# x normed ahead of everything, memory rows transposed beside the first output projection

## What is computed

```python
def rmsnorm(x, gain):
    y = x * rsqrt(mean(x * x, axis=-1, keepdims=True) + EPS) * gain

# block 1: gated recurrence heads (a) and forgetting attention heads (b)
h = rmsnorm(x, norm1_gain)
proj = h @ w_in                      # 2048 -> q_a, f_a, i_a, g_a, q_b, k_b, v_b, f_b
x = x + concat([o_a, o_b]) @ w_out   # "out"
h = rmsnorm(x, norm2_gain)
x = x + conv_ffn(h, ...)             # ffn0, down0, ffn1, down1
...
# block 2, both layers: 4-head cross attention into 256 fixed memory rows
mk, mv = split(mem @ w_mem_kv[layer], 2)
```

## Time and profile before

| | |
|---|---|
| median of 3 runs | 2035.94 us (2035.9 to 2038.04) |
| profiled execution | 2034.77 us |
| its span in the trace | 2033.1 us |
| TensorE busy | 2002.6 us |
| VectorE busy | 1239.8 us |
| ScalarE busy | 866.2 us |

### The profile page before, as it was taken

How to read it: one execution, slowest core, us unless ns; L and a number is a source line. 1 busy time by engine, 2 the same in 40 slices (tenths; PEclk the granted TensorE clock), 3 DMA queues, 4 the chain that set the end, 5 groups by cost and what they waited for, 6 DMA issues and landing times.

```text
span 2033.1 us, 24675 instructions
## 1 busy us (share of the span) xinstructions
PE 2002.6 (99%) x10731; PEld 1716.6 (84%) x10731; DVE 1239.8 (61%) x1113; ACT 866.2 (43%) x806; POOL 21.7 (1%) x62
## 2 busy tenths in 40 slices
PE   7999999999999999999999999999999999999998
PEld 6888987888888888888888888888878888888886
DVE  6665556655666664456666545657865864566665
ACT  5444344444544443344444435343344433344542
POOL 2000000000000000000000000000000000000000
PEclk9999999999999999999999999999999999999999
DMA  9755455475665655556555666746485656554552
GB/s 343 231 166 186 126 168 162 146 268 186 196 198 175 207 175 195 190 191 203 181 192 187 249 216 198 230 152 186 151 331 186 217 186 190 185 158 147 193 199 88
DMA packets 295288, 393.22 MB, mean 193 GB/s; under 512 B 6446, under 2 KB 225387, under 8 KB 293515
## 3 DMA queue, kind: packets, MB, share of 16 engines
q1 hardware_dynamic: 292320, 365.19, 55.4%
q0 software_dynamic: 2400, 26.28, 3.3%
q10 hardware_dynamic: 459, 0.16, 0.0%
HBM read 383.22 MB, written 8.39 MB: 193 GB/s over the span
## 4 chain that ended last, share of the span: by engine, by line
PE 93%; DVE 3%; ACT 1%; issue 1%; DMA 1%; SPq 0%; DVEq 0%; ACTq 0%
PE G L383 37%; PE G L387 18%; PE G L428 11%; PE G L430 11%; PE G L429 11%; PE SB L684 1%; DVE hl_ring L353 1%; ACT hl_ring L350 1%; DMA xt<-in_x 1%; PE OB L705 1%; DVE ytmp L634 0%; PE G L448 0%; PE G L450 0%; PE G L449 0%; DVE ringscr L1650 0%
## 5 line engine op out<-in xcount | busy, mean ns | idle before, releaser
L353 DVE TENSOR_TENSOR hl_ring<-raw,hl_ring 128x2048 fp32r<-128x2048 f32 (+1 forms) x348 | 783.9, 2256 | 521.0 <-ACT hl_ring L350 520.6
L350 ACT ACTIVATE hl_ring<-raw 128x2048 fp32r<-128x2048 f32 (+1 forms) x348 | 655.1, 1886 | 587.8 <-PE G L430 309.0
L383 PE MATMUL G<-ahl,hl_ring 128*128 128x512 f32 x2112 | 665.2, 396 | 0.0
L387 PEld LDWEIGHTS G<-ahl,hl_ring 128*128 128x128 f32 x2112 | 396.7, 188 | 93.7
L387 PE MATMUL G<-ahl,hl_ring 128*128 128x256 f32 x2112 | 415.1, 278 | 0.0
L383 PE MATMUL G<-ops,hl_ring 128*128 128x512 f32 x1216 | 384.3, 397 | 1.4 <-DVE hl_ring L353 1.4
L383 PEld LDWEIGHTS G<-ahl,hl_ring 128*128 128x128 f32 x2112 | 322.0, 189 | 0.8 <-issue 0.5
L387 PEld LDWEIGHTS G<-ops,hl_ring 128*128 128x128 f32 x1216 | 228.4, 188 | 53.9
L387 PE MATMUL G<-ops,hl_ring 128*128 128x256 f32 x1216 | 239.1, 278 | 0.0
L383 PEld LDWEIGHTS G<-ops,hl_ring 128*128 128x128 f32 x1216 | 185.6, 189 | 1.9 <-DVE hl_ring L353 1.6
L428 PE MATMUL G<-hl_ring,hhl 128*128 128x512 f32 x352 | 136.9, 389 | 0.0
(11 more groups left out here) (335 smaller groups left out, 1735.8 us busy)
## 6 DMA issues: line engine op xcount, KB each, us to landing
raw<-in_w_in SPq DMA_DIRECT2D x120, 1024.0 KB, 5.4
raw<-in_w_out SPq DMA_DIRECT2D x48, 1024.0 KB, 5.1
raw<-in_w_ffn_gate SPq DMA_DIRECT2D x44, 1024.0 KB, 5.1
raw<-in_w_ffn_up SPq DMA_DIRECT2D x44, 1024.0 KB, 5.1
raw<-in_w_ffn_down SPq DMA_DIRECT2D x40, 1024.0 KB, 5.1
raw<-in_w_kv_shared SPq DMA_DIRECT2D x24, 1024.0 KB, 5.2
raw<-in_w_mem_kv SPq DMA_DIRECT2D x16, 1024.0 KB, 5.2
ahl<-memop_scratch POOLq DMA_DIRECT2D x2, 4096.0 KB, 13.9
```

The costliest lines, as they stand in the source:

```text
L350: eng.activation(hi[:, s, 0:size], raw[:, r, 0:size], ACT.Copy).then_inc(hi_ready, 1)
L353: eng.tensor_tensor(lo[:, s, 0:size], raw[:, r, 0:size], hi[:, s, 0:size].bitcast(F32), ALU.subtract).then_inc(lo_ready, 1)
L383: eng.matmul(G[:, 2 * pair + b, :], hi[:, s, w], p.rhs(k), start=first and q == 0, stop=False)
L387: last = eng.matmul(G[:, 2 * pair + b, 0:TOK], lo[:, s, w], p.rhs(k)[:, 0, :], start=False, stop=final and q == len(ks) - 1)
```

## The change

x is loaded first, in three pieces with a semaphore each, and normed at once: ScalarE takes the squares and a square root in place of logarithm and exponential, VectorE scales the first half and the third quarter, ScalarE the last. The gain of the first norm alone is loaded by ScalarE's queue and transposed ahead; the other vectors come on GpSimd's queue and are transposed after the second tile of `in_f`. The first tile of the kernel is one of `in_f`; groups 4 to 7 of x are turned inside it, through a `hook` before every other step. Memory is loaded into `normx` once the forgetting attention has ended, transposed after the third and fourth tile of `out`, and `mem_k0` runs between `out` and `mem_v0`. The turned memory needs no way back for `mem_v0`.

```diff
-        add("mem_k0", 2, std(A["w_mem_kv"][0], 0), mem_ops)
         add("in_f", 4, std(A["w_in"], HG), act_ops)
...
         add("out", 4, full_source(A["w_out"], 0, (2, 3, 0, 1)), mixed, form="F", tpc=4, mats=turned_mats)
+        add("mem_k0", 2, std(A["w_mem_kv"][0], 0), mem_ops)
...
+            sp.dma_start(xt[:, 0, :], A["x"][0:P, :]).then_inc(x_loaded[0], 16)
+            for i in range(2):
+                w = slice(i * 1024, (i + 1) * 1024)
+                sp.dma_start(xt[:, 1, w], A["x"][P:2 * P, w]).then_inc(x_loaded[1 + i], 16)
+            for p in order:
                 sp_phase(sp, p.name)
...
+            pool.wait_ge(s_o, HH)
+            for t in range(TT):
+                pool.dma_start(normx[:, t, :], A["mem"][t * P:(t + 1) * P, :]).then_inc(mem_loaded, 16)
             pool.wait_ge(mem_lo, 8)
-            pool.wait_ge(tile_used, 2)
             pool.dma_start(memop, memhl[:, :, :, :].rearrange("p k h t -> p (k h t)")).then_inc(mem_saved, 16)
             phase_over(pool, "mem_k0")
             store(0, 0)
             pool.wait_ge(mem_saved, 16)
-            pool.wait_ge(r_lo, 4)
-            bring_back(memhl)
+            pool.wait_ge(stored, 16)
...
+            pe.wait_ge(x_scaled, 2)
+            pe_turn(pe, 0, 0)
...
+            def first_tile(k):
+                if k and k % 2 == 0:
+                    pe_turn_group(pe, 0, 3 + k // 2)
+                if k % 2 == 0:
+                    pe.wait_ge(t_lo, k // 2 + 1)
+
+            def beside_f(m):
+                if m == 0:
+                    pe_turn_group(pe, 0, 7)
+                if m == 1:
+                    pe.wait_ge(consts, 1)
+                    pe.wait_ge(vec_loaded, 10 * 16)
+                    for v, n in enumerate((124, 105, 88)):
+                        last = pe.transpose(XP[0][:, v * P:v * P + n], vrows[0:n, v, :], ident[0:n, 0:n])
+                    last.then_inc(vec_t, 1)
...
+            def beside_out(m):
+                if m not in (2, 3):
+                    return
+                if m == 2:
+                    pe.wait_ge(s_tmp, HH)
+                    pe.wait_ge(mem_loaded, 32)
+                for g in range(4 * (m - 2), 4 * (m - 2) + 4):
+                    if g >= 4:
+                        pe.wait_ge(mem_lo, g - 3)
...
+            act.wait_ge(x_loaded[0], 16)
+            act.activation(normx[:, 0, :], xt[:, 0, :], ACT.Square, accum_out=ssum[:, 0:1]).then_inc(x_square, 1)
+            act.wait_ge(x_square, 1)
+            act.activation(nrs[:, 0, 0:1], ssum[:, 0:1], ACT.Sqrt, scale=1.0 / D, bias=epsr[:, 0:1]).then_inc(x_root, 1)
...
             split(act, True, 0)
+            act.wait_ge(gain_ready, 1)
+            act_turn(act, 0, 0)
+            act_turn(act, 0, 4)
             split(act, True, 1)
...
             split(dve, False, 0)
...
+            dve.wait_ge(gain_ready, 1)
+            dve_turn(dve, 0, 0)
+            dve_turn(dve, 0, 4)
             split(dve, False, 1)
```

More of the change, by code:

```diff
@@ L379, in alternate @@
             for g in range(0, len(order), 2):
+                if hook is not None:
+                    hook(g // 2)
                 for (b, ks, width, col, first, final), q in order[g:g + 2]:
@@ L413, in pe_phase @@
                     if p.form == "A":
-                        last = alternate(eng, p, pair, s, c, t)
+                        last = alternate(eng, p, pair, s, c, t, hook if m == 0 else None)
                     for b, ks, width, col, first, final in p.mats(c, t) if p.form != "A" else ():
@@ L582, in dve_scale, with pe_turn_group @@
                 ins.then_inc(t_xn, 1)
+        def pe_turn_group(eng, u, g):
+            if u == 0 and g == 4:
+                eng.wait_ge(x_rest, 1)
+            if u and g == 0:
+                eng.wait_ge(t_xn, 2 * u)
+            if g >= 4:
+                eng.wait_ge(t_y if u == 3 else t_lo, g - 3 if u == 3 else 8 * u + g - 3)
+            for k in range(2):
+                for t in range(TT):
+                    kk = 2 * g + k
+                    last = eng.transpose(XP[g % 4][:, k * 256 + t * P:k * 256 + (t + 1) * P],
+                                         normx[:, t, kk * P:(kk + 1) * P], ident[:, :])
+            last.then_inc(t_t, 1)
         def pe_turn(eng, u, first):
             for g in range(first, first + 4):
[L587 to L596, removed]
+                pe_turn_group(eng, u, g)
         def act_turn(eng, u, first):
@@ L933, in _ @@
         def _(pe):
[L934 to L951, removed]
+            pe.wait_ge(ident_ready, 1)
+            pe.wait_ge(gain_loaded, 16)
+            pe.transpose(G[:, 3, 0:16], vrows[0:16, 0, :], ident[0:16, 0:16]).then_inc(gain_t, 1)
+            pe.wait_ge(x_scaled, 2)
+            pe_turn(pe, 0, 0)
             def turns(u):
@@ L962, in normed @@
                 return (((t_lo, 8 * u + 4),), ((t_lo, 8 * u + 8),))
-            pe_phase(pe, "mem_k0", between=turns(0))
-            pe_phase(pe, "in_f", halves=normed(0))
+            def first_tile(k):
[12 more added lines that the diff above has]
+                    last.then_inc(vec_t, 1)
+            pe_phase(pe, "in_f", between=beside_f, halves=((), ((t_lo, 8),)), hook=first_tile)
             pe_phase(pe, "in_q")
@@ L1121, in turns, with beside_f @@
                 return beside
[L1123 to L1132, removed]
+            def beside_f(m):
+                if m == 3:
+                    act.wait_ge(lb_chain, 3)
+                    act.activation(lbt[:, 2:4, :], lbt[:, 0:2, :], ACT.Exp).then_inc(lb_exp, 1)
+                    act.wait_ge(fw_loaded, 16)
+                    act.wait_ge(fw_zero, 2)
+                    for j in range(6):
+                        ins = act.activation(fwhi[:, :, j * HH:(j + 1) * HH], fwraw[:, :, :], ACT.Copy)
+                    ins.then_inc(fw_hi, 1)
+            cut_phase(act, True, "in_f", no_evict, between=beside_f)
             def beside_q(m):
@@ L1228, in _, with beside_out @@
                 act.activation(ah[:, 2 * b:2 * b + 2, :], ablk[:, 2 * b:2 * b + 2, :], ACT.Copy).then_inc(r_hi, 1)
-            cut_phase(act, True, "out", squares_evict(act, "out"))
+            def beside_out(m):
+                if m in (2, 3):
+                    for g in range(4 * (m - 2), 4 * (m - 2) + 4):
+                        act.wait_ge(in_t, g + 1)
+                        if g == 0:
+                            act.wait_ge(r_lo, 4)
+                        act.activation(memh[:, 2 * g:2 * g + 2, :], blocks(XP[g % 4]), ACT.Copy).then_inc(mem_hi, 1)
+            cut_phase(act, True, "out", squares_evict(act, "out"), between=beside_out)
             act_rstd(act, 1)
+            cut_phase(act, True, "mem_k0", no_evict)
             cut_phase(act, True, "mem_v0", full_evict(act, "mem_v0", mem_values), between=turns(1))
@@ L1560, in _, with beside_out @@
             lower(3)
-            cut_phase(dve, False, "out", residual_evict(dve, "out"))
+            def beside_out(m):
+                if m in (2, 3):
+                    for g in range(4 * (m - 2), 4 * (m - 2) + 4):
+                        dve.wait_ge(mem_hi, g + 1)
+                        dve.tensor_tensor(meml[:, 2 * g:2 * g + 2, :], blocks(XP[g % 4]),
+                                          memh[:, 2 * g:2 * g + 2, :].bitcast(F32), ALU.subtract).then_inc(mem_lo, 1)
+            cut_phase(dve, False, "out", residual_evict(dve, "out"), between=beside_out)
             dve_scale(dve, 1)
+            cut_phase(dve, False, "mem_k0", kv_evict("mem_k0"))
             cut_phase(dve, False, "mem_v0", no_evict, between=turns(1))
```

180 lines of the change are left out of this document (93 added, 87 removed).

## The result

The changed kernel takes 2045.51 us (median of 5 runs, 2041.92 to 2045.8), the kernel before 2035.94; the ratio is 1.004, 95% interval 1.0029 to 1.005. It is slower, by 9.6 us where 6.6 were forecast, and 0.2 us above the upper end of the range. Seven later runs of the unedited kernel had a median of 2043.0, 6.3 above the kernel before in the same session; the middle of all twelve is 2043.7. So the five recorded runs lie in the upper part of the changed kernel's spread. The profiled execution took 2045.51 with a span of 2043.8, 10.7 more than before.

A forecast was written before the change was run, and what follows sets the result against it. TensorE was taken as the bound. Second tile done at 39.2, plus 22.3, 3.5 and 0.4 owed, less 11.1 for two `in_f` tiles, gives 54.3; less 47.7 is +6.6 us, so 2042.5, range 2039.2 to 2045.3 (+3.3 to +9.4).

The forecast's parts named there:

- the clock's own end: Upper end for the second tile's clock loss: 1.6 us, where 0.8 was taken between 0 and 1.6.
- The landing and the first matmul: At the start, x and the first weight tile land, are normed, cut and turned; first matmul at 18.8, against 18.04.
- the lag: Delay from data moved to usable, 1.6 us on the old first weight tile, assumed again for x and that tile.
- The first tile: First `in_f` tile with 16 transposes of x: 7.3 us, plus 1.6 for half clock, ending at 27.7.
- The wait behind the first tile: TensorE idles 5.1 us before the second `in_f` tile, whose cut stands behind all eight turned groups.
- the three steps named: After the first tile, in sequence: ScalarE's copy of the last group 0.9, ScalarE's second cut 1.9, VectorE's 2.3 us.
- The second tile: Second `in_f` tile: starts at 32.8, 5.57 us plus 0.8 of clock, done at 39.2.
- The owed work: Still due after the second tile: four `mem_k0` tiles 22.3, 32 memory transposes 3.5, vectors' transposes 0.4 us.
- after 1400 the same 16.8 us: Sign expected in the changed profile: TensorE idle after 1400 us stays at 16.8 us.
- Rival 2: Clock kept and loads early at the start, x and tile without lag: +2.6 us, 2038.5; chance 0.14.
- Rival 3: Turning hidden, second cut over by about 25, second tile done at 30.7: -1.9 us, 2034.0; chance 0.04.
- Rival 4: Weights late in `out` under the memory load and write: +12 us, 2048; chance 0.04.

The follow-up runs named there:

- after_hold_out0: Changed kernel with 22 identity transposes in TensorE's wait before the kernel's second output projection ("the projection"): 2042.28 us, ratio 1.0025.
- hold_second: Changed kernel with 40 identity transposes behind the first tile's last turned group, filling TensorE's wait for the second tile: 2041.58 us, ratio 1.0024.
- after_all_hold: Changed kernel with 60 and 28 identity transposes around x's first transposes, 40 before the second tile, 22 before the second output projection: 2038.92 us, ratio 1.0011.
- before_hold_out0: Kernel before the change with 22 identity transposes in TensorE's wait before the kernel's second output projection: 2035.33 us, ratio 0.9995.
- cut2_between: Changed kernel with ScalarE's and VectorE's second weight cut moved between the fourth and fifth turned group of x: 2038.61 us, ratio 1.0013.
- cut2_paced: As cut2_between, and the second tile waits for turned groups one by one instead of all eight at once: 2037.34 us, ratio 1.0002.
- paced_warm: cut2_paced with identity transposes in three waits: 60 before x's first transposes, 28 behind them, 22 before the second output projection: 2033.46 us, ratio 0.9984.
- before_all_hold: Kernel before the change with 14 and 26 identity transposes around the vectors' transposes and 22 before the second output projection: 2036.98 us, ratio 1.0.

## Why the prediction was right, and where a size was off

**The verdict and its cause.** Right in the direction and in the mechanism; the recorded median lies 0.2 us above the range. The change is slower because TensorE, the bound, starts its second tile late and has 3.5 us of transposes more to pay; both are shown by edits that undo or double them. The range itself was loose: its upper end, +9.4, has no row behind it, as the clock's own end gives 6.6 + 0.8 = 7.4.

**The landing and the first matmul**: forecast 18.8, measured 17.96. x came earlier than the lag allowed for: ScalarE's first square starts at 5.91, not 7.2, and the first weight tile is taken at 12.79, not 13.7. The new load moved 221 GB/s until 6 us and 329 until 9, where the old one, with eight small pieces in front, moved 195 and 299; whether the pieces are the reason was not tested. By its own rows, the prediction's 5.6 and 7.2 for the first half should also have been 5.4 and 7.0. The estimate that the prediction took from the Trainium skill ("DMA: Bandwidth & Descriptors") had the tile at 11.6, so the trace lies between the two. Its 2 us stand there, in the section on the anatomy of a DMA, for loads on GpSimd's path, and this load is on SP's queue.

**The first tile**: 7.3 us of work and 1.6 of clock were forecast, 10.1 measured (17.96 to 28.1), so 2.8 of clock. The old first tile as a row for the clock was mis-sized, since how long the half rate lasts is not the same from start to start: in after_hold_out0 the same tile took 9.2, and in hold_second 7.4.

**The wait behind the first tile**: forecast 5.1, measured 5.05, by the three steps named.

**The second tile**: forecast 5.57 and 0.8 of clock, measured 7.48 (33.14 to 40.62), so 1.9. The half that I took between 0 and 1.6 was too little, and 1.6 was no upper end. In after_hold_out0 the tile took 7.00, so 1.4 of clock.

**The owed work**: 3.5 for the memory transposes, 3.5 measured for as many again. All owed work came to 26.4 where 26.2 was summed: 8.0 behind at 40.62, 8.2 at the projection. The memory loads and the 4 MB write moved at nothing: from 40 to 1400 us TensorE idles 0.4 us.

**What was left out**: "after 1400 the same 16.8 us" held for the idle and not for the time. The fall of the clock at the projection, 2.5 us at the end of the profiled execution, was in no term, because one profile of before without it was taken for what always happens, in spite of runs of before that spread by 2 us. In the profiled executions the distance from 6.6 to 10.7 is this 2.5 and 1.6 at the start and in the owed work.

**What was luck**: the start's errors are -0.8, +1.2 and +1.1 in the profiled execution, so one hides part of the other two. That 6.6 is near the 7.0 between the two kernels with the projection held is in part a draw of the clock: the profiles of that pair differ by 1487.12 - 1480.40 = 6.7, because the clock lost less at both tiles there. The 9.6 of the recorded five is as much an upper draw: the later session had 6.3 with nothing held.

**The rivals.** Rival 2 needed a clock kept everywhere, and after_all_hold is that case: +3.6 on before_hold_out0 (2038.92 against 2035.33), where 6.6 - 2.4 = +4.2 follows without earlier loads; they came 0.8 earlier. Rival 3's point, the second cut over by about 25 us, is what cut2_between and cut2_paced bring about (VectorE ends it at 22.4 in both), and cut2_paced came out even with the kernel before. Its sum had the second tile done at 30.7 at full clock and the kernel 1.9 faster; in paced_warm that tile is done at 31.05, and the kernel is 1.9 faster than before_hold_out0. Rival 4 did not occur.

What stays open is how often the clock falls at each of the three places, and whether it falls at the projection as often in the kernel before as in the change; profiles of single executions show where, and the timed runs only the sum.

## What to carry to other kernels

When a chain is started earlier, look at what its own engines were asked to do in between: here ScalarE and VectorE finished the whole turning before they cut the second tile, and moving one line on each gave back about 5 us of the median. Work that leaves an idle stretch for a saturated one is paid in full, however small it looks; price it where it lands. When two kernels differ by a few microseconds and TensorE has waits of 2 to 5 us, fill those waits with harmless transposes in both before comparing: the spread of the change fell from 4 us to 0.6. Look in the trace where the filled time goes, though: in before_all_hold it came back in the next wait, and that kernel still spreads by 2.4 us.

## What the runs showed of the hardware that I had not expected

The same wait of 2.79 us before the same projection let the clock fall in one execution (1.00 at 1486, 0.50 at 1490) and left it at full in another. Of the eight profiled executions without spins there, seven show the fall. Transposes of the identity, about 0.11 us each (28 of them take 3.22 us in paced_warm), kept it at full in all five that had them there.

The granted clock that the profile gives for the first microseconds did not fit the matmuls there. In the changed kernel it reads full at 18 us:

```profile
18.00:19.00 1.00, 1.00 (x3) 0.81 (x4) 1.00 (x4) 0.00 (x0) 0.81 (x1) 1.00 1.10 344
```

while two steps of the first tile start at 17.96 and 19.38, 1.42 us apart, as at half rate; in paced_warm they are 0.77 apart (18.01 and 18.78). The duration of the matmuls tells the rate there, not the column.

An idle filled in front of a wait for data moves the wait, and can move the fall of the clock with it, as before_all_hold shows.
